# Turning latent queries and keys by block transposes and transfers, and scaling the products with V at the end, in a two-block transformer kernel

## The reference, cut to what matters

```python
q = (rms_norm(c_q, q_norm) @ w_uq).reshape(B, S, H, QK_NOPE_DIM + QK_ROPE_DIM)   # 8 heads x (64 + 32)
q_nope, q_pe = q[..., :QK_NOPE_DIM], rope(q[..., QK_NOPE_DIM:], pos_f)
kv = (rms_norm(c_kv, kv_norm) @ w_ukv).reshape(B, S, H, QK_NOPE_DIM + V_HEAD_DIM)
k_nope, v = kv[..., :QK_NOPE_DIM], kv[..., QK_NOPE_DIM:]
k_pe = rope(k_pe_raw[:, :, None, :], pos_f)[:, :, 0]
s = (jnp.einsum('bqhd,bkhd->bhqk', qn, k_nope).astype(jnp.float32)
     + jnp.einsum('bqhr,bkr->bhqk', qp, k_pe).astype(jnp.float32))
p = jax.nn.softmax(s * MLA_SCALE, axis=-1)
return jnp.einsum('bhqk,bkhd->bqhd', p.astype(v.dtype), v)
```

## Time and profile before

| what | value |
|---|---|
| median of 3 runs (lowest, highest) | 1026.31 us (1025.63, 1026.74) |
| the profiled execution | 1026.88 us |
| its span, first to last instruction | 1025.1 us |
| mean granted TensorE clock | 0.998 of full speed |
| busy: PE, weight loads of PE, DVE, ACT, POOL | 99%, 82%, 67%, 55%, 14% |
| DMA | 204.61 MB, 200 GB/s on average |
| the chain of waits that ended last | 93% PE |

### The profile page before, as it was taken

How to read it: one execution, slowest core, us unless ns; L and a number is a source line. 1 busy time by engine, 2 the same in 40 slices (tenths; PEclk the granted TensorE clock), 3 DMA queues, 4 the chain that set the end, 5 groups by cost and what they waited for, 6 DMA issues and landing times.

```text
span 1025.1 us, 14271 instructions
## 1 busy us (share of the span) xinstructions
PE 1015.6 (99%) x4764; PEld 836.6 (82%) x4764; DVE 686.6 (67%) x1041; ACT 564.4 (55%) x923; POOL 140.7 (14%) x219
## 2 busy tenths in 40 slices
PE   9999999999999999999999999999999999999997
PEld 6999888888877778888888888888887688888886
DVE  6777865646688985656568565656788785655643
ACT  6665654545567764444556454454676854454542
POOL 1001450000143253000014000000400221000002
PEclk9999999999999999999999999999999999999999
DMA  9574567566643467657576665757653455756551
GB/s 369 187 243 168 195 222 240 183 221 206 207 144 125 145 226 251 224 195 239 180 232 195 231 214 191 244 175 243 200 184 124 146 184 182 245 184 231 195 168 46
DMA packets 109694, 204.61 MB, mean 200 GB/s; under 512 B 57472, under 2 KB 62992, under 8 KB 109648
## 3 DMA queue, kind: packets, MB, share of 16 engines
q1 hardware_dynamic: 107472, 198.55, 57.9%
q0 software_dynamic: 1888, 5.17, 1.6%
q10 hardware_dynamic: 288, 0.31, 0.1%
HBM read 187.20 MB, written 1.05 MB: 184 GB/s over the span
## 4 chain that ended last, share of the span: by engine, by line
PE 93%; DVE 3%; DMA 1%; ACT 1%; SPq 1%; POOL 0%; issue 0%; POOLq 0%; DVEq 0%; ACTq 0%
PE pG L2185 16%; PE pG L2177 16%; PE pG L2181 16%; PE pD L2177 11%; PE pD L2181 11%; PE pD L2185 11%; PE pG L2158 2%; PE pG L2160 1%; PE pG L2164 1%; PE pT L2194 1%; DVE w_low L1735 1%; DMA h<-in_x 1%; PE pD L2158 1%; PE pD L2164 1%; PE pD L2160 1%; PE pT L2379 1%
## 5 line engine op out<-in xcount | busy, mean ns | idle before, releaser
L1735 DVE TENSOR_TENSOR w_low<-raw,w_high 128x1024 fp32r<-128x1024 f32 x339 | 408.9, 1226 | 181.4 <-ACT w_high L1424 171.3
L1424 ACT ACTIVATE w_high<-raw 128x1024 fp32r<-128x1024 f32 x340 | 353.5, 1056 | 192.1 <-PE pG L2185 134.4
L2177 PE MATMUL pG<-w_high,xTh 128*128 128x512 f32 x712 | 219.8, 390 | 0.0
L2185 PE MATMUL pG<-w_low,xTh 128*128 128x512 f32 x712 | 219.4, 389 | 0.2 <-DVE w_low L1735 0.2
L2181 PE MATMUL pG<-w_high,xTl 128*128 128x512 f32 x712 | 219.3, 389 | 0.0
L2185 PEld LDWEIGHTS pG<-w_low,xTh 128*128 128x128 f32 x712 | 133.6, 188 | 28.3 <-DVE w_low L1735 0.6
L2181 PEld LDWEIGHTS pG<-w_high,xTl 128*128 128x128 f32 x712 | 133.5, 188 | 28.0 <-DVE xTl L1795 0.2
L2177 PEld LDWEIGHTS pG<-w_high,xTh 128*128 128x128 f32 x712 | 133.2, 188 | 27.5
L1531 ACT ACTIVATE gate<-pG,stat 128x256 f32<-128x256 f32 x102 | 48.4, 474 | 151.8 <-PE pG L2185 135.9
L2177 PE MATMUL pD<-w_high,aTh 128*128 128x512 f32 x348 | 107.8, 391 | 0.0
L2181 PE MATMUL pD<-w_high,aTl 128*128 128x512 f32 x348 | 107.4, 390 | 0.1
(11 more groups left out here) (318 smaller groups left out, 1113.0 us busy)
## 6 DMA issues: line engine op xcount, KB each, us to landing
raw<-in_stream SPq DMA_DIRECT2D x340, 512.0 KB, 4.3
aF<-aB SPq DMA_DIRECT2D x320, 32.0 KB, 2.5
post<-in_posts POOLq DMA_DIRECT2D x5, 512.0 KB, 5.9
early<-in_stream SPq DMA_DIRECT2D x4, 512.0 KB, 12.5
xF<-hg SPq DMA_DIRECT2D x32, 64.0 KB, 2.5
xF<-hg POOLq DMA_DIRECT2D x32, 64.0 KB, 2.2
h<-in_x SPq DMA_DIRECT2D x2, 512.0 KB, 11.6
first_w<-in_opening SPq DMA_DIRECT2D x2, 384.0 KB, 4.2
```

Of the source, the lines that this page charges most:

```text
L1424: sc.activation(w_high[:, slot(static):slot(static) + CHUNK], raw_of(static), ACT.Copy).then_inc(w_high_done, 1)
L1735: ve.tensor_tensor(w_low[:, slot(static):slot(static) + CHUNK], raw_of(static), w_high[:, slot(static):slot(static) + CHUNK].bitcast(F32), ...
L2177: pe.matmul(dst, ah, w_high[:, where:where + n], start=start, stop=False)
L2185: mm = pe.matmul(dst, ah, w_low[:, where:where + n], start=False, stop=stop)
```

## The change

- `MT` is gone. `MB(t)` on DVE turns mq and mk in blocks of 32x32, two instructions of 128x768, into post and into mk_turned. `MV(t)` moves the blocks to mqT and mkT: 8 transfers per tile of 96 KB, SP issues 4 and POOL 4. The columns of w_uq and w_ukv are put in another order on the host, so that a head's 96 features come to lie on partitions. mkT is now read in pieces of 32 numbers.
- `MB(1)` and `MV(1)` stand right behind `U(1)`. All of r_v and the first chunk of r_g of tile 0 come ahead of `MS(0)`: nine chunks where there were four. The rounds keep one chunk in each of rounds 1, 3, 5 and 7.
- `MN` is gone: mp stays as it is, and `MPT` waits for `ME` alone. `ML(t)` is new: POOL takes lsum to the power -1 for all 8 heads of a tile and spreads each over 64 columns (weights_wide), PE turns these 128x512 numbers with 4 transposes into the half of pD[1 - t] that is free, and ACT copies them to heads_cat. `MAT(t)` on DVE now multiplies the products with V by heads_cat. `CAT(t)` does what `MAT` did, from heads_cat. `ML(0)` stands in round 4 and `ML(1)` behind `MPT(7)`.
- `RV` is split: SP issues 4 transfers per tile and POOL 4. `RV(1)` and the third `decay` stand elsewhere in round 7.

The lines of code that are left out rename semaphores, move junk and let waits stand on the new names.

```diff
@@ -631,7 +631,8 @@
     for c in range(1, 4):
         project(1, 1, c)
     refill(step, freed, 2)
-    step("MT", 0)
+    step("MB", 0)
+    step("MV", 0)
     refill(step, freed, 2)
     step("KPE", 1)
     for c in range(4):
@@ -639,55 +640,60 @@
         if c in (1, 2):
             refill(step, freed, 1)
     step("U", 1)
+    step("MB", 1)
+    step("MV", 1)
     step("exp_table",)
     step("RROPE", 1, 0)
     refill(step, freed, 1)
     freed += [C_U, C_U + 1, C_U + 2]
     projects(3, 0, range(2))
-    step("MT", 1)
     refill(step, freed, 1)
     behind_maxima = freed.pop(0) + RING
     step("high", behind_maxima)
     projects(3, 0, range(2, 4))
+    for c in range(4):
+        project(3, 1, c)
+    step("low", behind_maxima)
+    project(4, 0, 0)
     step("MS", 0)
-    step("low", behind_maxima)
     step("ME", 0)
     step("RB", 0, 0)
     step("RB", 0, 1)
-    beside = [(3, 1, c) for c in range(4)] + [(4, 0, c) for c in range(4)] + [(4, 1, 0)]
-    project(*beside.pop(0))
-    project(*beside.pop(0))
+    beside = [(4, 0, 1), (4, 0, 2), (4, 0, 3), (4, 1, 0)]
     for v in range(1, 8):
-        step("MN", v - 1)
         step("MS", v)
         if v in (1, 3):
             refill(step, freed, 1)
         step("ME", v)
+        if v == 7:
+            step("RV", 1)
+        if v % 2:
+            project(*beside.pop(0))
         if v in (3, 5, 7):
             step("MPV", v - 3)
             step("MPV", v - 2)
-        project(*beside.pop(0))
         step("MPT", v - 1)
         if v == 2:
             step("VC", 0)
         if v == 4:
+            step("ML", 0)
             step("RV", 0)
             step("RROPE", 1, 1)
         if v == 5:
+            step("MAT", 0)
             step("RSUM",)
             step("RB", 1, 0)
         if v == 6:
             step("RB", 1, 1)
         if v == 7:
-            step("RV", 1)
             step("VC", 1)
-        if v in (2, 4, 6):
-            step("decay", v // 2 - 1)
-    step("MN", 7)
+        if v in (2, 4, 7):
+            step("decay", v // 2 - 1 if v < 7 else 2)
     refill(step, freed, 2)
     project(4, 1, 1)
     step("MPT", 7)
-    step("MAT", 0)
+    step("ML", 1)
+    step("CAT", 0)
     step("gate", 0)
     for hd in range(3, 6):
...
@@ -697,6 +703,7 @@
     step("RS", 0)
     step("RM", 0)
     refill(step, freed, 1)
+    step("MAT", 1)
     project(4, 1, 3)
     step("decay", 6)
...
@@ -712,7 +719,7 @@
     step("RM", 2)
     refill(step, freed, 1)
     output(0, 1)
-    step("MAT", 1)
+    step("CAT", 1)
     step("RPV", 2)
     step("RS", 3)
     step("RM", 3)
...
         post = place("post", [P, D], F32)
+        weights_wide = place("weights_wide", [P, 512], F32, at[0])
+        heads_cat = [place("heads_cat", [P, 512], F32, at[0] + 2048)[:], post[:, 0:512]]
...
+        mk_turned = place("mk_turned", [P, MLA_HEADS * QK], F32, junk_at)
...
@@ -1181,13 +1194,23 @@
                     sp.dma_start(xF[t][:, first + 128 * a:first + 128 * a + 128],
                                  hg[t][32 * a:32 * a + 32, first:first + 512]).then_inc(hF_moved[half], 16)
 
+            def MV(t, ph):
+                sp.wait_ge(mB_ready, 2 * t + 1)
+                for a in range(0, 2):
+                    sp.dma_start(mqT[:, t, :, a, :], post[32 * a:32 * a + 32, 0:MLA_HEADS * QK]).then_inc(m_moved, 16)
+                sp.wait_ge(mB_ready, 2 * t + 2)
+                for a in range(0, 2):
+                    sp.dma_start(mkT[:, t, a, :, :], mk_turned[32 * a:32 * a + 32, :]).then_inc(m_moved, 16)
+
             def RV(t, ph):
                 sp.wait_ge(ms_psum, 4 * (t + 1))
+                if t == 1:
+                    sp.wait_ge(rT_moved, 64)
                 for part in range(2):
                     sp.wait_ge(rB_ready, 2 * t + part + 1)
-                    for a in range(4):
+                    for a in range(0, 2):
                         dst = rkT[:, t, :, a, :] if part else rqT[:, t, a, :, :]
-                        sp.dma_start(dst, block_turned(t, part)[32 * a:32 * a + 32, :]).then_inc(rT_moved[t], 16)
+                        sp.dma_start(dst, block_turned(t, part)[32 * a:32 * a + 32, :]).then_inc(rT_moved, 16)
...
+
+            def ML(t, ph):
+
+                pool.wait_ge(mp_ready, 8 * (t + 1))
+                if t == 1:
+                    pool.wait_ge(wide_psum, 1)
+                link(pool.tensor_tensor(lrec[t][:, 0:MLA_HEADS], lsum[t][:, 0:MLA_HEADS], one_neg[:, 0:MLA_HEADS], ALU.pow))
+                pool.tensor_copy(weights_wide[:].rearrange("p (a f) -> p a f", f=HD),
+                                 lrec[t][:, 0:MLA_HEADS].unsqueeze(2).broadcast_to([P, MLA_HEADS, HD])).then_inc(wide_ready, 1)
...
+            def MV(t, ph):
+                pool.wait_ge(mB_ready, 2 * t + 1)
+                for a in range(2, 4):
+                    pool.dma_start(mqT[:, t, :, a, :], post[32 * a:32 * a + 32, 0:MLA_HEADS * QK]).then_inc(m_sent, 16)
+                pool.wait_ge(mB_ready, 2 * t + 2)
+                for a in range(2, 4):
+                    pool.dma_start(mkT[:, t, a, :, :], mk_turned[32 * a:32 * a + 32, :]).then_inc(m_sent, 16)
+
...
+            def ML(t, ph):
+                sc.wait_ge(wide_psum, t + 1)
+                if t == 1:
+                    sc.wait_ge(rT_moved, 64)
+                    sc.wait_ge(rT_sent, 64)
+                sc.activation(heads_cat[t], pD[1 - t][:, 512:1024], ACT.Copy).then_inc(wide_copied, 1)
+
+            def CAT(t, ph):
                 x_product(sc, 4, t)
-                sc.wait_ge(mpv_done, 4 * (t + 1))
-                sc.activation(xTh[t][:, 0:4, :].rearrange("p k r -> p (k r)"), pD[t][:, 512:1024], ACT.Copy).then_inc(cath_ready[t], 1)
+                sc.wait_ge(cat_ready, t + 1)
+                sc.activation(xTh[t][:, 0:4, :].rearrange("p k r -> p (k r)"), heads_cat[t], ACT.Copy).then_inc(cath_ready[t], 1)
...
+            def MB(t, ph):
+
+                ve.wait_ge(mqk_ready, 2 * t + 2)
+                if t == 1:
+                    ve.wait_ge(m_moved, 64)
+                    ve.wait_ge(m_sent, 64)
+                ve.transpose(post[:, 0:MLA_HEADS * QK], mq[:]).then_inc(mB_ready, 1)
+                ve.wait_ge(u_out, 4 * t + 3)
+                ve.transpose(mk_turned[:], mk[:]).then_inc(mB_ready, 1)
...
-            def MN(v, ph):
-                t, j = v // 4, v % 4
-                ve.wait_ge(mp_ready, 2 * (v + 1))
-                chain(ve.reciprocal(lrec[t][:, 2 * j:2 * j + 2], lsum[t][:, 2 * j:2 * j + 2]))
-                joined()
-                ve.tensor_tensor(mp[v % 2][:], mp[v % 2][:], lrec[t][:, 2 * j:2 * j + 2].unsqueeze(2).broadcast_to([P, 2, SEQ]),
-                                 ALU.mult).then_inc(mn_ready, 1)
...
+                ve.wait_ge(mpv_done, 4 * (t + 1))
+                ve.wait_ge(wide_copied, t + 1)
+                ve.tensor_tensor(heads_cat[t], pD[t][:, 512:1024], heads_cat[t], ALU.mult).then_inc(cat_ready, 1)
+
+            def CAT(t, ph):
                 ve.wait_ge(cath_ready[t], 1)
-                ve.tensor_tensor(xTl[t][:, 0:4, :].rearrange("p k r -> p (k r)"), pD[t][:, 512:1024],
+                ve.tensor_tensor(xTl[t][:, 0:4, :].rearrange("p k r -> p (k r)"), heads_cat[t],
...
-            def MT(t, ph):
-                pe.wait_ge(mqk_ready[t], 2)
-                for i, src in enumerate((mq, mk)):
-                    if i == 1:
-                        pe.wait_ge(u_out, 4 * t + 4)
-                    for hd in range(MLA_HEADS):
-                        mm = turned((pG, pT)[hd // 4][i][0:QK, hd % 4 * P:(hd % 4 + 1) * P], src[:, hd, :])
-                    mm.then_inc(mT_psum, 1)
...
             def MS(v, ph):
                 t, j = v // 4, v % 4
                 if v == 0:
                     for r in range(2):
-                        pe.wait_ge(mqT_ready, 2 * r + 2)
-                        pe.wait_ge(mkT_ready, 2 * r + 2)
+                        pe.wait_ge(m_moved, 64 * (r + 1))
+                        pe.wait_ge(m_sent, 64 * (r + 1))
+                    pe.wait_ge(u_out, 8)
                 if v >= 2:
                     pe.wait_ge(mp_ready, 2 * (v - 1))
                 for x in range(2):
                     hd = 2 * j + x
-                    mm = pe.matmul(pG[v % 2][:, SEQ * x:SEQ * (x + 1)], mqT[:, t, hd, :], mkT[:, hd, :],
+                    mm = pe.matmul(pG[v % 2][:, SEQ * x:SEQ * (x + 1)], mqT[:, t, hd, :, :].rearrange("p a j -> p (a j)"), mkT[:, :, :, hd, :],
                                    start=True, stop=True)
                 mm.then_inc(ms_psum, 1)
...
             def MPT(v, ph):
-                pe.wait_ge(mn_ready, v + 1)
+                pe.wait_ge(mp_ready, 2 * (v + 1))
...
+            def ML(t, ph):
+                pe.wait_ge(wide_ready, t + 1)
+                if t == 1:
+                    pe.wait_ge(cat_ready, 1)
+                for j in range(4):
+                    mm = turned(pD[1 - t][:, 512 + P * j:512 + P * (j + 1)], weights_wide[:, P * j:P * (j + 1)])
```

(10 more changed lines are left out.)

81 lines of the change are left out of this document (42 added, 39 removed).

## The result

The changed kernel takes **1034.46 us** in the median (7 runs, 1031.52 to 1040.01); the kernel before, on the same chip, takes 1025.76 us (7 runs, 1025.50 to 1026.74). The ratio is 1.0091, 95% interval 1.0074 to 1.0107: 8.7 us slower. I had forecast 1030.1 us and a range up to 1034.0. The sign is right, the size less than half, and the result lies just outside the range. The profiled execution took 1035.39 us, 8.51 more than that of before, and its span is 8.5 us longer.

A forecast was written before the change was run, and what follows sets the result against it. PE, busy 99% of the span, was taken as the bound. Work of 24.4 plus waits of 7.2 put RS(0) 3.8 us later; on the profiled 1026.88 that gives 1030.7, less 0.57 for the median: 1030.1 us, range 1027.6 to 1034.0.

The forecast's parts named there:

- The sign: Whole kernel: the change was forecast to be slower, RS(0) 3.8 us later; chance of slower 0.77.
- Step 1, MT: Ahead of MS(0): removing MT(0) gains 0.8 us, PE waiting 0.95 at X(2, 1, 0); MT(1) gives its whole 1.76.
- Step 1, MV: Ahead of MS(0): transfers to mqT and mkT land by 773.4, 1.0 us before MS(0), so they cost nothing.
- the rival: MS(0) waits for MV(1): POOL's issues 1 us slower each than SP's cost 3 us, giving 1033; chance 0.07.
- Three terms at nothing: In the sum: MV's transfers cost 0, no fall of the clock, and nothing for the program's end.
- ML's two waits: PE waits for POOL's weights_wide 2.4 us at ML(0) and 4.0 us at ML(1).
- Step 2, the rounds: MS(0) to RS(0): PE work of 24.4 us plus waits of 7.2 gives 31.6, with RS(0) at 806.1.
- a sum of 5.0: ML(1)'s copy on POOL could wait 1.22 us more for a low part on DVE: 5.0 instead of 3.8.
- a rival with 0.15: The clock falls while PE waits, as in ML(1)'s wait of 4.0: 1031.5 to 1033.5 us; chance 0.15.
- The faster rival: PE hardly waits for ML: without any such wait a shift of -2.2 us, 1024.1; chance 0.09.
- No wait for rT: Before RS(0): RV(1), issued from two queues, is no longer waited for, a gain of 1.0 us.
- the unchanged stretch behind RS(0): Behind RS(0) PE's list is the same, so the shift of 3.8 us stays to the end.

The follow-up runs named there:

- experiment 13: Experiment 8 with X(2, 1) moved to the free second half of pD[1], ScalarE's copy staying in place: 1024.41 us, ratio 0.9987 to the kernel before.
- experiment 5: The changed kernel with all sixteen transfers that it gave to POOL (in MV and RV) back on SP: 1036.42 us.
- experiment 2: The changed kernel with the keys (mk) turned and their transfers sent ahead of the queries' (mq): 1034.13 us.
- experiment 3: The changed kernel with the edits of experiment 1 and experiment 2 together: 1027.98 us.
- experiment 9: The kernel before with only the new scaling (MN gone, ML added); MT, RV on SP and a chunk in every round stay: 1027.56 us.
- experiment 12: The changed kernel with POOL's VC(1) and its part of decay(2) put behind ML(1) instead of ahead of it: 1029.89 us.
- experiment 4: The changed kernel with 30 transposes without use on PE in the wait before ML(1): 1032.99 us.
- experiment 10: Experiment 8 with X(2, 1) moved to bank pG[1] and copied by ScalarE before U(1): 1033.11 us.
- experiment 11: Experiment 10 with the transfers of half 0 (mkT and mqT) all on SP: 1032.39 us.
- experiment 6: The changed kernel with 20, 16 and 30 transposes without use on PE before MS(0), ML(0) and ML(1): 1034.01 us.
- experiment 1: The changed kernel with PE's transposes and ACT's copy of ML moved later, POOL's power and copy staying in place: 1028.42 us.
- experiment 7: Experiment 3 with MAT(0) later, PE's and ACT's ML(1) right behind RS(0), and Oc(0, 0) no longer waiting for MAT(1): 1026.42 us, ratio 1.0009.
- experiment 8: Experiment 7 with RV's transfers all on SP, eight of them taken back from POOL: 1026.34 us.

## Why the prediction was right and wrong

- **Step 1, MT.** Right: "It starts at 753.2", with 0.95 of waiting, was 753.25 with 0.78 by the profile. I had called it a gain of 0.8 and stopped there; experiment 13 shows that the other 0.8 was to be had by another bank.
- **Step 1, MV: the failed step.** "So all is there by 773.4 ... MV costs nothing." MS(0) waited 2.31, until 777.1. The term that was too small is the landing. DVE's second block of half 1 was ready at 767.4, as summed (767.2), and the last issues were under way at 768.9, no later than summed, but the landing of mkT's transfers took 4.5 to 8.2 us, not the 3.59 that I took from RV(1). RV(1)'s transfers have 64 KB and ran in an emptier stretch (DMA share 0.47 between 798 and 802, before). The DMA engines were full here (page of the stretch 760 to 775 us, after):

```profile
DMA packets 4543, 4.36 MB, mean 291 GB/s; under 512 B 3223, under 2 KB 3600, under 8 KB 4542
q1 hardware_dynamic: 4160, 3.57, 85.7%
q0 software_dynamic: 382, 0.78, 21.2%
```

  Before, the same stretch had 896 packets and a share of 62.3%. In experiment 5, where mkT's transfers left later, they landed much sooner, though they are the same transfers. From issue to landing, of mkT in the change and then in experiment 5:

```profile
DMA to landing us min/median/max: 4.5/5.2/8.2
DMA to landing us min/median/max: 2.1/2.2/2.3
```

  The share of the DMA engines was 1.01 between 775 and 777 in the change and 0.71 between 775 and 778 in experiment 5. This fits a landing that grows with the load; no run changes the load alone. I had written the rival down, with its cause in POOL's slow issues (they took 0.56 to 0.88 us, like SP's) and a chance of 0.07. The place was right, the cause was the landing.
- **Three terms at nothing.** The transfers (2.31), the clock (1.5 to 1.7) and the end (0.83) are what the sum lacks in the profiled execution, 4.6 to 4.8 us together; ML's two waits came out 0.8 shorter than summed, and small pieces before MS(0) and in the rounds make up for that. The transfers are the largest there, but not surely in the median: where experiments 2 and 3 took the wait before MS(0) away, the medians fell by only 0.3 and 0.4. How the median's 4.4 us above the forecast divide stays open.
- **Step 2, the rounds.** The chain was nearly exact: POOL's power began 24.93 behind MS(0) (forecast 24.9), PE wanted it at 24.65 (24.6), and the waits were 0.52, 0, 1.97 and 3.65 (forecast 0.65, 0.1, 2.4, 4.0). Two mistakes cancelled in ML(1): the power took 1.67, not 2.55, the copy 1.58, not 1.04. The 0.14 for two semaphores, for which I named no row, was 0.12 to 0.13 in the change's timelines. And I read the queue ahead of the power as given; experiments 9 and 12 show that it, with the copy's meeting DVE, was 3.1 of the 3.65.
- **Who interferes.** The Trainium skill (SBUF — State Buffer, Who interferes with whom) was used for a sum of 5.0. The runs agree with it: POOL's copy of 128x512 took 0.61 to 0.71 where no low part was running when it began (in experiment 9 it began 0.14 us ahead of one, and DVE's pair took 2.68 instead of 2.36) and 1.58 to 1.61 where it began within one; in experiment 12 VC(1) and the product behind it met the low parts: the product of 128x128 took 1.44 instead of 0.45 and DVE's pair 3.19. The power fits as well: the 2.55 that I took from the kernel before began 0.16 us into a low part, while ML(1)'s began 0.48 ahead of one (802.02 and 802.50) and took 1.67. So the long price was for the wrong case. Who begins first seems to keep its time; that is what I read from these four meetings, not a test of it.
- **The clock.** Not in the sum, and a rival with 0.15. It fell in the profiles of the change and of experiments 2, 4, 5, 10 and 11, each time behind or within a wait of PE of 1.97 to 6.3 us, and never with the waits filled (6) or none over 1.3 us (1, 3, 7, 8, 9, 13); in experiment 12 a wait of 1.97 brought none. One fall costs 1.5 to 1.7. It probably also makes most of the spread (experiment 6). The Trainium skill (TensorE: Matmul & The Clock Gate, HAM oscillation) describes such repeated falls for waits on transfers; here waits for GpSimd do it, so a wait of this length should carry the price of a fall in the sum.
- **The end of the program.** No step had it: 0.83 us for sixteen transfers given to POOL.
- **A slip in a rival.** The faster rival's turning point, waits of 2.6 in all, needs a power and a copy in 1.2 us, not in 1.8: the two waits are that time less 0.32 and that time plus 0.44. That speaks further against the rival. The result lies well on the other side.
- **No wait for rT** and the unchanged stretch behind RS(0) were right (216.16 and 216.17).

The cases were alternatives in my text, each with a chance of its own, but three of them came true together: the forecast's waits, the transfers and the clock. A range made of one case at a time was too narrow for that.

## What to carry to other kernels

Before a step goes to a nearly idle engine, list what stands ahead of it in that engine's queue and what the neighbour on its port does just then: here the order and the neighbour were 3.1 us of a 3.65 us wait, and 0.3 to 0.5 were left without them. Put the wait for such a result where the waiting engine has other work: that move alone (experiment 1) gave 6.0 of the 10.0 us between the change, which cost 8.7, and experiment 13, which with six more moves gained 1.5 (ratio 0.9987). And price transfers by ones from a stretch with the same load, not by those of a quiet one.

## What the runs showed of the hardware

- GpSimd's last drain took 3965 to 3967, 4288, 4613 to 4615 and 5267 to 5268 ns with 0, 4, 8 and 16 transfers more on its queue than the kernel before: 81 ns each. It counts only where it ends behind SP's wait for the last store: not with 4 more (end 6.58), by some 0.2 us with 8 (6.81 and 6.85), by 0.8 to 0.9 with 16 (7.43 to 7.49).
- ML's power of 128x8 on GpSimd took 1.65 to 1.79 us in all kernels. A power of the same size in the kernel before took 2.55 where it began 0.16 us behind a low part on DVE, and 1.64 where none ran.
- The granted clock fell behind PE's wait of only 1.97 us in the profiles of experiments 2, 4 and 5, and not behind the same wait in those of the change and of experiment 12; in experiment 5 it did not fall behind the 3.65 us before ML(1). The length of the wait alone doesn't decide. What does is open.
- The start of the program moves by 2.2 us between profiles of kernels that are equal there, so single profiles are compared from a common instruction on.
